# Attention, gating and 32 experts on one core: the output projection in token halves, one more chunk prefetched, and the last pieces smaller

## The reference, cut to what matters

```python
xn = rms_norm(h, attn_norm); proj = xn @ w_in
o_a = mla_branch(...)                       # 8 heads
o_b = diff_branch(...)                      # 4 heads, two softmaxes each
merged = sigmoid(gate_a) * (o_a @ w_branch_mla) + sigmoid(gate_b) * (o_b @ w_branch_diff)
h = h + merged @ w_out                      # the output projection
t = rms_norm(h, ffn_norm)
logits = t @ w_router + b_router            # 32 experts, the best 4 of each token
for e in range(32):
    u = t @ w1[e] + b1[e]                   # 1024 x 2048
    a = glu * sigmoid(1.702 * glu) * (lin + 1.0)
    out = out + gates[:, e:e + 1] * (a @ w2[e] + b2[e])   # 1024 x 1024
```

## Time and profile before

| | us |
|---|---|
| median of 3 runs | 1157.66 (1156.36 to 1158.23) |
| the profiled execution, device time | 1157.1 |
| its span, first to last instruction | 1155.2 |
| TensorE busy | 1107.6 |
| VectorE, ScalarE, GpSimd busy | 303.5, 206.9, 36.1 |

### The profile page before, as it was taken

One profiled execution on the slowest core, in us unless ns is written; L12 is line 12 of the kernel. 1 busy time (PEld: TensorE's weight loads), 2 busy tenths in 40 slices (PEclk: granted clock), 3 DMA queues, 4 the chain that ended last, 5 costly groups with the idle time before them and its releaser, 6 DMA issues.

```text
span 1155.2 us, 12817 instructions
## 1 busy us (share of the span) xinstructions
PE 1107.6 (96%) x5124; PEld 513.3 (44%) x5124; DVE 303.5 (26%) x552; ACT 206.9 (18%) x355; POOL 36.1 (3%) x44
## 2 busy tenths in 40 slices
PE   8999999999999999999999898989898999999997
PEld 8867788744343434343434242424242424242422
DVE  4566766521211111121211111111111202020212
ACT  6646565411010101010100000000000101010100
POOL 1005310000000000000000000000000000000000
PEclk9999999989999999999999999999999999999999
DMA  9654237799999999999999999999999999999997
GB/s 368 268 182 145 74 110 295 299 414 371 406 427 421 427 428 428 428 431 427 428 428 428 431 427 428 428 428 431 427 428 428 428 431 427 428 428 429 428 427 289
DMA packets 34542, 439.10 MB, mean 380 GB/s; under 512 B 3984, under 2 KB 4112, under 8 KB 6704
## 3 DMA queue, kind: packets, MB, share of 16 engines
q1 hardware_dynamic: 33840, 433.55, 90.0%
q10 hardware_dynamic: 672, 5.12, 1.1%
HBM read 437.60 MB, written 1.05 MB: 380 GB/s over the span
## 4 chain that ended last, share of the span: by engine, by line
PE 73%; DMA 24%; ACT 2%; DVE 1%; issue 1%; SPq 0%; ACTq 0%; DVEq 0%
DMA ring<-in_expert_w 24%; PE bank L742 20%; PE bank L765 20%; PE bank L424 12%; PE bank L717 5%; PE bank L690 5%; PE bank L643 4%; PE bank L407 3%; PE bank L474 1%; PE bank L510 1%; PE bank L485 1%; DMA tok_r<-in_x_turned 0%; PE bank L715 0%; PE bank L535 0%; ACT gate_r L976 0%
## 5 line engine op out<-in xcount | busy, mean ns | idle before, releaser
L742 PE MATMUL bank<-ring,feat_r 128*64 128x512 f32 x1504 | 334.5, 596 | 9.7 <-DMA ring<-in_expert_w 9.7
L742 PEld LDWEIGHTS bank<-ring,feat_r 128*64 128x64 f32 x1504 | 103.2, 137 | 231.6 <-issue 206.8
L765 PE MATMUL bank<-ring,late_r 128*64 128x512 f32 x768 | 173.3, 596 | 12.4 <-DMA ring<-in_expert_w 12.0
L424 PE MATMUL bank<-ring_s,feat_s 128*128 128x512 f32 (+2 forms) x448 | 136.8, 388 | 2.5 <-DVE ring_s L1138 2.3
L1392 DVE TENSOR_SCALAR gate_r<-bank 128x512 f32<-128x512 f32 x32 | 22.1, 692 | 433.2 <-PE bank L742 433.2
L742 PE MATMUL bank<-pool_r,feat_r 128*64 128x512 f32 x512 | 114.6, 595 | 9.5 <-DMA pool_r<-in_expert_w 9.5
L1414 DVE TENSOR_TENSOR acc_r<-bank,acc_r 128x512 f32<-128x512 f32 x64 | 44.3, 692 | 259.7 <-PE bank L717 259.7
L1082 ACT ACTIVATE gate_r<-gate_r 128x512 f32<-128x512 f32 x32 | 20.2, 630 | 482.3 <-DVE gate_r L1392 482.3
L765 PEld LDWEIGHTS bank<-ring,late_r 128*64 128x64 f32 x768 | 54.0, 137 | 117.5 <-issue 114.9
L424 PEld LDWEIGHTS bank<-ring_s,feat_s 128*128 128x128 f32 x448 | 81.5, 191 | 17.5 <-issue 5.0
L424 PE MATMUL bank<-ring_s 128*128 128x512 f32 (+2 forms) x224 | 84.9, 379 | 0.0
(11 more groups left out here) (187 smaller groups left out, 598.5 us busy)
## 6 DMA issues: line engine op xcount, KB each, us to landing
ring<-in_expert_w SPq DMA_DIRECT2D x140, 2048.0 KB, 31.3
pool_r<-in_expert_w SPq DMA_DIRECT2D x48, 2048.0 KB, 33.0
ring<-in_head_w SPq DMA_DIRECT2D x23, 1024.0 KB, 5.0
ring<-in_head_w SPq DMA_DIRECT2D x7, 768.0 KB, 9.2
ring<-in_expert_w SPq DMA_DIRECT2D x4, 1024.0 KB, 33.5
gate_r<-in_expert_w ACTq DMA_DIRECT2D x1, 2048.0 KB, 9.0
late_r<-in_expert_w ACTq DMA_DIRECT2D x1, 2048.0 KB, 14.7
ring<-in_head_w SPq DMA_DIRECT2D x2, 576.0 KB, 15.0
```

The source lines that it names most:

```text
L424: mm = pe.matmul(banks[m][:, 0:cols], featT[left][:, first + k, m * P:(m + 1) * P], right[:, k - k0, :], start=(k == 0 and left == 0 and r ...
L742: mm = pe.matmul(b[e * SLOTS:(e + 1) * SLOTS, :], xT[:, k, e * SLOTS:(e + 1) * SLOTS], w[:, e, g, :], start=False, stop=(k == KD - 1), ski ...
L765: mm = pe.matmul(bank[4 + h][e * SLOTS:(e + 1) * SLOTS, :], aT[k // 4][:, k % 4, e * SLOTS:(e + 1) * SLOTS], w[:, q, e, :], start=(k == 0) ...
```

## The change

- The second half of the output projection is done for the first 128 tokens, then for the others. The norm, the turn, the router, the choice and the gather are done for each token half as it comes. The turn now takes `acc` itself. The gain is folded into the router weights (one GpSimd instruction) and into the copy of the gathered tokens, which moves from ScalarE to VectorE (`xT_copy`). A broadcast load of 512 KB goes away.
- `ONCE` is (1, 3, 6): chunk 1 is loaded into `qkT_r`, which held turned queries and keys. Chunk 6 is issued at the end of attention instead of after the router.
- The first bias lies in four groups of 32 rows, 512 columns each, with the selection matrix `pick` repeated in each. The first `start_u` moves from ahead of the first gather to the middle of the first up projection.
- The last down projection is loaded in nine pieces: seven of 1 MB, two of 0.5 MB.
- `WARM` is 40.

```diff
 DOUBLE = 2 * SLOT
 EXTRA = 2
 WIDE = RING // 2 + EXTRA
-ONCE = (3, 6)
-PIECES = 4
-WARM = 28
+WARM = 40
 FIRST = None
 
...
+        spare = pool_r[:, 2 * DOUBLE:2 * DOUBLE + 3 * NM * P]
+        onehot = spare[:, 0:NM * P].rearrange("p (m e s) -> p m e s", m=NM, e=2)
+        gated = spare[:, NM * P:2 * NM * P].rearrange("p (m e s) -> p m e s", m=NM, e=2)
+        gatedT = spare[:, 2 * NM * P:]
         xT = v3(feat_r[:, 0:KD * P], KD)
...
 
         extra = [pool_r[:, 0:DOUBLE], pool_r[:, DOUBLE:2 * DOUBLE]]
...
             load_pair(0, 2 * last, last)
-            load_pair(1, 2 * last + 1, last, JOB_CHUNKS - 2)
-
-
-            for q in range(PIECES):
-                n = NHEAD + CYCLE * last + 2 * JOB_CHUNKS - 2 + q // 2
-                if q % 2 == 0:
+            load_pair(1, 2 * last + 1, last, PIECES[0][0])
+
+
+            for q, (c, k, nk) in enumerate(PIECES):
+                n = NHEAD + CYCLE * last + JOB_CHUNKS + c
+                if k == 0:
                     sp.wait_ge(ring_used, n - WIDE + 1)
-                c = slice((q % 2) * SLOT, (q % 2 + 1) * SLOT)
-                sp.dma_start(slot(n)[:, c], expert_w[PAIRS - 1, JOB_CHUNKS - 2 + q // 2, :, c]).then_inc(sem(f"piece_landed{q}"), 16)
+                part = slice(k * D, (k + nk) * D)
+                sp.dma_start(slot(n)[:, part], expert_w[PAIRS - 1, c, :, part]).then_inc(sem(f"piece_landed{q}"), 16)
...
+
+            pool.wait_ge(sem("small_landed"), 16)
+            pool.tensor_tensor(v3(w_rt, KD), v3(w_rt, KD), g_ffn.unsqueeze(2).broadcast_to([P, KD, E]), ALU.mult)\
+                .then_inc(sem("router_scaled"), 1)
 
...
             pe.wait_ge(sem("featT_ready"), 8)
             split_product((bank[0], bank[1]), (n + 1,))
-            split_product((bank[2], bank[3]), (n + 2, n + 3))
-
-            def start_u(f, j):
+            wr = v3(w_rt, KD)
+
...
+
+            split_part((bank[2], bank[3]), n + 2, range(KD // 2), (0,))
+            split_part((bank[2], bank[3]), n + 3, range(KD // 2, KD), (0,))
+            h_turn(0, 0)
+            h_turn(0, 1)
+            split_part((bank[2], bank[3]), n + 2, range(KD // 2), (1,))
+            h_turn(1, 0)
+            split_part((bank[2], bank[3]), n + 3, range(KD // 2, KD - 2), (1,))
+            pe.wait_ge(sem("router_scaled"), 1)
+            pe.wait_ge(sem("tT_copied"), 3)
+            part_logits(0, slice(0, SEQ))
+            part_logits(1, slice(0, P)).then_inc(sem("partials"), 1)
+            split_part((bank[2], bank[3]), n + 3, range(KD - 2, KD), (1,))
+            pe.wait_ge(sem("tables_ready"), TABLES)
+            logits(0)
+            h_turn(1, 1)
+            pe.wait_ge(sem("chosen"), 1)
+            pe.matmul(bank[2][:, 0:E], before[:], chosen_v[:, 0], start=True, stop=True, skip_group_check=True)\
+              .then_inc(sem("places"), 1)
+            pe.matmul(bank[3][:, 0:E], ones[:], chosen_v[:, 0], start=True, stop=False, skip_group_check=True)
+            pe.wait_ge(sem("tT_copied"), 4)
+            part_logits(1, slice(P, SEQ)).then_inc(sem("partials"), 1)
+            pe.wait_ge(sem("t_scaled"), 1)
+            pe.wait_ge(sem("first_onehot"), 1)
+            first_gather(0, (0, 1))
+            logits(1)
+            first_gather(0, range(2, 6))
+            pe.wait_ge(sem("chosen"), NM)
+            pe.matmul(bank[3][:, 0:E], before[:], chosen_v[:, 1], start=False, stop=True, skip_group_check=True)\
+              .then_inc(sem("places"), 1)
+            first_gather(0, range(6, KD))
+            pe.wait_ge(sem("t_scaled"), NM)
+            pe.wait_ge(sem("onehot_ready"), 1)
+            first_gather(1, range(KD))
+
+            def start_u(f, j, start=True):
 
                 pe.wait_ge(sem("pick_ready"), j + 1)
                 for g in range(2):
-                    c0 = g * F + f * HALF
-                    pe.matmul(bank[2 * f + g][:], pick.rearrange("p e s -> p (e s)"), b1_sb[:, c0:c0 + HALF],
...
-            pe.matmul(bank[2][:, E:2 * E], before[:], chosen_v[:, 1], start=False, stop=True, skip_group_check=True)\
-              .then_inc(sem("places"), 1)
+                    q = slice((2 * g + f) * E, (2 * g + f + 1) * E)
+                    pe.matmul(bank[2 * f + g][:], pick[q].rearrange("p e s -> p (e s)"), b1_sb[q, :],
+                              start=start, stop=False, skip_group_check=True)
 
             def weights_turn():
...
                         for g, b in enumerate((bank[2 * f], bank[2 * f + 1])):
                             for e in range(2):
                                 mm = pe.matmul(b[e * SLOTS:(e + 1) * SLOTS, :], xT[:, k, e * SLOTS:(e + 1) * SLOTS],
-                                               w[:, e, g, :], start=False, stop=(k == KD - 1), skip_group_check=True)
+                                               w[:, e, g, :], start=(late and k == 0), stop=(k == KD - 1),
+                                               skip_group_check=True)
+                        if late and k == 3:
+                            pe.wait_ge(sem("b1_landed"), 16)
+                            start_u(0, j, False)
                         if k % 2:
                             mm.then_inc(ring_used, 1)
...
 
             act.wait_ge(sem("scores"), SUB + HA)
-            act.dma_start(b1_sb, b1).then_inc(sem("bias_landed"), 16)
-            act.dma_start(b2_sb, b2).then_inc(sem("bias_landed"), 16)
+            load_expert_chunk(act, NHEAD + ONCE[0], ONCE[0], 0)
+            act.wait_ge(sem("ob_ready"), NM)
+            act.dma_start(b1_sb, b1).then_inc(sem("b1_landed"), 16)
             act.wait_ge(sem("valued"), SUB + HA)
-            act.dma_start(g_ffn, gain(ffn_norm, D)).then_inc(sem("ffn_gain_landed"), 16)
+            act.wait_ge(sem("o_turned"), 2)
+            load_expert_chunk(act, NHEAD + ONCE[-1], ONCE[-1], 0)
 
...
             split_hi(27)
 
             def tT_copy(i):
...
+                if i == 3:
+                    act.wait_ge(ring_used, chunk_index("w_out", 4, HALF) + 1)
                 act.copy(tT[:, 4 * h:4 * h + 4, m * P:(m + 1) * P], v3(bank[4 + i][:], 4)).then_inc(sem("tT_copied"), 1)
 
-            for h in range(2):
-                if h:
-                    tT_copy(0)
...
+            t_scale(0)
+            h_square(1, 1)
             tT_copy(3)
-            act.wait_ge(sem("h_summed"), 1)
-            act.activation(ssq[:, 54:56], ssq[:, 54:56], ACT.Sqrt, bias=eps[:], scale=1.0 / D).then_inc(sem("h_rooted"), 1)
-
-            act.wait_ge(sem("h_inverted"), 1)
-            for m in range(NM):
-                act.activation(t_sb[:, m], t_sb[:, m], ACT.Copy, scale=rstd[:, 54 + m:55 + m]).then_inc(sem("t_scaled"), 1)
-            act.wait_ge(sem("hg_ready"), 4)
-            act.wait_ge(sem("h_squared"), 4)
-            load_expert_chunk(act, NHEAD + ONCE[1], ONCE[1], 0)
-
-            def xT_copy(j, b0):
-
-                for i in range(2):
-                    act.wait_ge(sem("gathered"), 2 * j + i + 1)
-                    act.copy(xT[:, 4 * i:4 * i + 4, :], v3(bank[b0 + i][:], 4)).then_inc(sem("xT_copied"), 1)
-
-            xT_copy(0, 6)
...
+            dve.wait_ge(ring_used, chunk_index("w_out", 4, 0) + 1)
+            h_add(0, 0)
+            h_add(0, 1)
+            dve.wait_ge(sem("ob_ready"), NM)
+            dve.tensor_copy(pick, eye[:, 0:2].unsqueeze(2).broadcast_to([P, 2, SLOTS])).then_inc(sem("pick_ready"), 1)
+            dve.wait_ge(sem("h_squared"), 2)
+            ts(ssq[:, 56:58], ssq[:, 50:52], 1.0 / D, EPS, ALU.mult, ALU.add).then_inc(sem("h_biased"), 1)
+            dve.wait_ge(sem("h_first"), 1)
+            h_add(1, 0)
+
+            def h_invert(m):
+                dve.wait_ge(sem("h_rooted"), m + 1)
+                dve.reciprocal(rstd[:, 54 + m:55 + m], ssq[:, 54 + m:55 + m]).then_inc(sem("h_inverted"), 1)
+
+            def partial_copy(m):
+                dve.wait_ge(sem("partials"), m + 1)
...
 
-            dve.wait_ge(sem("places"), 1)
-            for m in range(NM):
-                stt(place_v[:, m, 0:E], bank[2][:, m * E:(m + 1) * E], FAR, chosen_v[:, m], ALU.add, ALU.mult)\
+            def first_onehot(m):
+
+                dve.wait_ge(sem("places"), m + 1)
+                dve.wait_ge(sem("chosen"), m + 1)
...
-                ins = tt(onehot[:, m], iota_b, spread(place_v[:, m, 0:2]), ALU.is_equal)
-            ins.then_inc(sem("onehot_ready"), 1)
+                tt(onehot[:, m], iota_b, spread(place_v[:, m, 0:2]), ALU.is_equal)\
+                    .then_inc(sem("onehot_ready" if m else "first_onehot"), 1)
+
+            def xT_copy(j, b0):
+
+                for i in range(2):
+                    dve.wait_ge(sem("gathered"), 2 * j + i + 1)
+                    tt(xT[:, 4 * i:4 * i + 4, :], v3(bank[b0 + i][:], 4),
+                       g_ffn[:, 4 * i:4 * i + 4].unsqueeze(2).broadcast_to([P, 4, P]), ALU.mult).then_inc(sem("xT_copied"), 1)
+
+            h_invert(0)
+            partial_copy(0)
+            dve.wait_ge(ring_used, chunk_index("w_out", 4, HALF) + 1)
```

(8 more changed lines are left out.)

218 lines of the change are left out of this document (109 added, 109 removed).

## The result

| | before | after |
|---|---|---|
| median, runs side by side | 1157.16 (1156.36 to 1158.23) | 1151.02 (1150.16 to 1151.78) |
| the profiled execution, device time | 1157.1 | 1151.78 |
| its span | 1155.2 | 1149.9 |

The ratio is 0.994, 95% interval 0.9926 to 0.9954: faster by 0.5 to 0.7%. The medians differ by 6.1 us, the two profiled spans by 5.3. Forecast was 8 to 9 us (1149.0, range 1145.5 to 1153.5).

The account below looks back on a forecast made before the run. Bound: weight transfers at 428 GB/s after a last pause set by TensorE. Router -6.8, first bias +0.3, warm-up -1.5, tail -1.3 sum to -9.3 us: 1148.4, raised to 1149.0 for unseen hand-overs; range 1145.5 to 1153.5.

Parts of the forecast that it names:

- The end follows TensorE's entry into pairs 1 and 2: Chunks 20 and 32 wait for TensorE's first use of pairs 1 and 2; the end moves one to one with it.
- The router section: From the end of `w_out` to the first expert matmul: token halves bring that matmul 6.8 us earlier, bounds 5.3 and 7.7.
- my lower bound: Router gain of only 5.3 us: first-half steps delay the second half's on VectorE by 1.5 us.
- The first bias: `start_u` moved into the up projection: cost 0.3 us; +1.9 with no overlap, -1.2 with full overlap.
- my slots: `start_u`'s two matmuls of two passes overlap only partly: three slots of four, so 1.5 us instead of 1.91.
- The warm-up: 12 extra transposes before the first product keep the clock up: -1.5 us, not taken up by a load; bounds 0 and -1.6.
- The tail: Last pair: with 1 MB pieces TensorE needn't wait for all of chunk 8; all behind moves -1.3 us, bounds -0.5 and -1.4.
- The extra chunk: One more chunk loaded ahead: value 0, as chunks 20 and 32 still wait for chunks 12 and 24.
- Rival 2: The 2 MB loaded ahead count in full and the last transfer pause is gone: 1141 us; chance 0.05.
- Rival 3: Router section gains only 3 instead of 6.8 us, token halves in series on VectorE and ScalarE: 1152.2 us; chance 0.13.
- Rival 4: Slower: `xT_copy` ahead of the `acc` additions on VectorE lengthens each pair: 1176 us; chance 0.02.
- Rival 1: TensorE's clock falls again around or behind the router, costing 2 to 3.5 us: 1151.7 us; chance 0.22.

Follow-up runs that it names:

- experiment 3: Changed kernel without the third buffer: chunk 1 goes through the ring instead of the turned queries' buffer; 1151.25 us, ratio 0.9943.
- experiment 6: Changed kernel with chunk 13 also put in the turned queries' buffer once chunk 1 is used, later ring chunks moving up one place; 1147.81 us, ratio 0.9921.
- Experiment 4: Changed kernel with both first-bias matmuls in one group of 32 rows, needing two more 64 KB loads; 1151.9 us, ratio 0.9945.
- experiment 1: Changed kernel with 28 warm-up transposes instead of 40; 1151.3 us, ratio 0.9938.
- experiment 5: Changed kernel with the third chunk of the first product split before the two squares of x instead of behind them; 1149.94 us, ratio 0.9932.
- experiment 12: The kernel of experiment 5 once more, unaltered, for a second profile; one run of 1149.36 us.
- experiment 11: The changed kernel once more, unaltered, for a second profile; one run of 1151.76 us.
- experiment 9: Changed kernel with 60 warm-up transposes instead of 40; 1151.21 us, ratio 0.9942.
- experiment 10: Changed kernel with the edits of experiment 5, experiment 6 and experiment 9 together; 1147.56 us, ratio 0.9912.

## Why the prediction was right, and where its sizes were off

**The end follows TensorE's entry into pairs 1 and 2: right.** Experiments 3 and 6 show it from both sides: 2 MB more that leave chunk 20's wait as it is are worth nothing, 2 MB that let chunk 20 go one chunk earlier are worth 2 to 3 us. Only "one to one" was too simple. Chunk 20 landed 7.9 us after its issue before and 9.9 to 10.4 in the changed kernel's two profiles.

**The router section, forecast -6.8, measured -6.0** (6.64 at the first expert matmul, less 0.66 by the warm-up). `w_out` ended where the sum had it: 224.98, and 225.6 without the warm-up's part, against 225.5. From there to the first expert matmul it is 8.1 us instead of 7.4. The step that failed is "work that stays beside it: the first half's choice on VectorE, its gather on TensorE". The second choice begins 3.78 us behind `w_out`, where the sum had 2.9 (0.65, 0.85, 0.5, 0.35, 0.55) and a few hand-overs. In between the rows show TensorE with the first half's places (0.63 us, and they wait for the first choice) and a piece of its gather (0.68 us), both ahead of what the second half waits for. So the first half did stand in the way, in TensorE's queue more than in VectorE's: the copy of the last turn is done at 227.03 and its product starts at 227.35, the partial copy is done at 228.13 and its fold starts at 228.42. These two make 0.6 of the 0.8 us, less than half of the 1.5 in my lower bound. This is read from the rows; no experiment took the first half's steps away. The last half of the gather took 2.02 us where the sum had 1.8.

**The first bias, forecast +0.3: the mis-sized term was `start_u`,** taken as 1.5 us and measured at 1.06, full overlap. From the first expert matmul to chunk 20's issue are 58.28 us instead of 58.77, so it gained 0.5 where the sum had a cost of 0.7 at this place (1.06 - 2 x 0.85 = -0.64 instead of 1.5 - 2 x 0.4). Experiment 4 shows that the row groups are the cause. The Trainium skill, "TensorEngine Tiling (Array Packing)", section "Key Properties", says that different tiles can execute weight loads and matmuls in parallel. The trace agrees, now for rows as well: 1.06 us, where my slots gave 1.5. By that rule the prediction had -1.2, which is 1.0 - 2 x 0.9 for chunk 20, less the 0.4 us that chunk 32 waited longer. That 0.4 was too small: it was taken from SP's issues, and the landings before show 1.0 (5.9 us from chunk 31 to chunk 32 instead of 4.9).

**The warm-up, forecast -1.5, measured -0.66 to -0.73** (the changed kernel, experiment 1). The clock did stay up (1.00 in 10 to 11 us), although the transposes ended at 8.66 and not at 10.1: 1.6 us idle before the first product, where before the change 2.3 us idle stood ahead of the half clock. The step that failed is "so the gain is not taken up by a load": the chain of before held TensorE in one piece only because TensorE was slow; once faster, it met the split behind the load of `x`. Experiments 5 and 12 give 0.80 to 0.85 more, and 0.66 + 0.85 is the 1.5.

**The tail, forecast -1.3, measured -0.9** with the data at their usual time (22.36 against 23.27 or 23.28). The sum let "all behind it" move by the same; there are 0.4 us of wait for chunk 10 left, since the pieces land no sooner in all. In the changed kernel's own profile a late piece took 1.4 more.

**The extra chunk, 0: right** (experiment 3). **Rival 2,** 1141: wrong, the dip is there. **Rival 3,** serial halves: a small part of it, the 0.8. **Rival 4:** wrong, a pair takes TensorE 1.7 us less. **Rival 1,** the clock falls again: it does, in 5 of the 13 profiles with the new router section. But it costs 0.7 to 1.1 us instead of the 2 to 3.5 in my price, since it ends at 231 to 233, under the gather or just behind it, and the experts hardly feel it. The Trainium skill, "TensorE: Matmul & The Clock Gate", section "What's actually happening", says that the default state is throttled and that activity releases it. The traces agree in where the falls are, behind the short gaps in which TensorE waits for VectorE (0.65 and 0.38 us between 225 and 227 in the changed kernel's rows). Experiments 5 and 12 add that the same instructions have the fall in one execution and not in another. In executions without a profile a fall may cost more: in experiment 6 the two with a mean granted clock of 0.998 took 1149.47 and 1149.70 us, the four with 0.999 or 1.000 1146.73 to 1147.82. Where their clock fell isn't on record.

**The sum again, with what was measured at chunk 20:** -6.0 - 0.5 - 0.66 = -7.2, the shift of its issue (7.1). Its landing is 1.9 us less, chunk 21's 1.1 less; the pause before chunk 32 that vanished gives 1.0, the delay at chunk 25 takes 1.3, which comes to 5.7 (5.9 at chunk 32's landing). The tail is 0.5 longer in this profile, and the span 5.3 us shorter. The median gains 6.1. So 1149.0 was 2 us too low, by the warm-up, the tail and the landing; the 0.8 that the router section lacked and the 0.8 or more that `start_u` gave cancel. The late single landings are partly luck: experiment 11 has neither the one at chunk 25 nor the one in the tail, one at 1078 us instead, and the same span.

**What stays open.** Why chunk 20 lands 2 us later after its issue. It is not that SP waited longer: chunk 20 is issued 2.1 us before chunk 19 lands (291.36 and 293.50) and still lands 7.7 us behind it; before the change 1.3 us (298.49 and 299.78) and 6.6. It isn't the buffer either: in the changed kernel chunk 20 goes to `pool_r` and before to `ring`, but in experiment 3 it goes to `ring` and lands 9.6 us after its issue. One more difference was seen: in the changed kernel a packet of the instruction queue falls into this stretch (here 290 to 298 us), where the kernel before has none until 308:

```profile
q1 hardware_dynamic: 179, 2.67, 89.2%
q8 instruction: 1, 0.02, 1.5%
```

It is a single packet, which took 1.9 us here, and a chunk counts as landed only when the last of the 16 counts of its semaphore has come. That the packet delays chunk 20 is argued and not shown, as experiment 9 failed to move the packet away. Some rows speak against it: in experiment 3 the packet took half as long (1.0 us), and chunk 20 was as late; in experiments 6 and 10 chunk 22, issued at 298.36 and 298.91, landed 10.0 and 7.6 us later, with the packet long past, at 293.6 and 292.6 us. Whether the late pieces and chunk 25's delay have the same cause wasn't tried either.

## What to carry to other kernels

Find the last pause of the bounding transfers, ask which use the transfer behind it waits for, and value each edit by how far it moves that use; a buffer counts only if it moves it too, and the next pause then caps the gain. When a stretch of one engine gets faster, look at what the other engines do at its end, not whether it was in one piece before: it will meet the next load. Of an edit worth under 1 us the issue time of one fixed transfer tells more than the time of the whole, and a second profile of the same kernel tells which of the differences are the edit's.

## What was unexpected in the hardware

- Two float32 matmuls with 32 rows, in different row groups and banks, take 1.06 us together and 1.91 in one group. Each instruction takes 0.6 to 0.7 in both, but in two groups they start in pairs, within 0.01 us of each other, and in one group 0.4 to 0.5 us apart.
- The clock fell at 228 us in one execution (0.50 at 229 to 230) and stayed at 1.00 in another of the same kernel.
- Single landings come 1.1 to 1.6 us late, and all behind them stay late by that. In the changed kernel's profile it was chunk 25 and a piece at 1134 us; in eight of the other twelve profiles with the new router section it was one chunk between 1077 and 1104 us. The cause is open. Two profiles of the changed kernel had the same span, 1149.9, by different ways.
- The same forty transposes took 5.93, 7.23 and 7.47 us in three executions (the changed kernel, experiments 3 and 11), and sixty took 8.80 and 9.20 (experiments 9 and 10). TensorE does 6 to 8 of them in a microsecond at first and 12 later, and the step comes at 5 to 6 us in the changed kernel's profile and at 7 in experiment 9's, while the granted clock reads 1.00 for both rates. So the 0.74 us between the 28 before and the 40 after was not the price of twelve.
